# All weight blocks multiplied unsplit from a landing ring of eight, in a two-layer transformer kernel in 32-bit floats

## What is computed

```
x = layer_norm(ALPHA * x + s5_mixer(x), ...)              # state-space mixer with a scan over 256 steps
kv = shared_kv(x, ...)                                    # keys, values, two compressed branches
x = layer_norm(ALPHA * x + nsa_mixer(x, ..., kv), ...)    # 16 heads, 3 attention branches, gates
for l in range(2):
    h = rms_norm(x, g_mix)
    x = x + (retention_na_mixer(h) if l == 0 else diff_attention_mixer(h))
    x = x + cross_attention(rms_norm(x, g_x), memory)     # 4 heads, 256 memory rows
    gate, up = split(rms_norm(x, g_ffn) @ w_ffn_in)       # 2048 -> 2 x 5632
    x = x + (silu(gate) * up) @ w_ffn_out                 # 5632 -> 2048
```

## Time and profile before

| | |
|---|---|
| median of 3 runs | 3734.83 us (3734.79 to 3744.37) |
| the profiled execution's own time | 3741.45 us |
| its span, first to last instruction | 3739.7 us |
| TensorE busy (PE) | 3589.8 us, 96% |
| VectorE busy (DVE) | 2219.3 us, 59% |
| ScalarE busy (ACT) | 1654.8 us, 44% |
| mean granted TensorE clock | 0.983 of 2.4 GHz |
| read from memory | 607.85 MB, 163 GB/s over the span |

### The profile page before, as it was taken

The page is one execution under the profiler, slowest core; times in us unless marked ns, Lnnn a source line. Parts: engine busy times, 40 slices in busy tenths (PEclk is TensorE's granted clock), DMA queues, the critical chain, the costliest instruction groups (busy, mean ns, idle before and its releaser), DMA issues.

```text
span 3739.7 us, 48011 instructions
## 1 busy us (share of the span) xinstructions
PE 3589.8 (96%) x20133; PEld 3082.5 (82%) x20133; DVE 2219.3 (59%) x2922; ACT 1654.8 (44%) x2278; POOL 233.1 (6%) x236
## 2 busy tenths in 40 slices
PE   7888999999999999899999999999989999999999
PEld 6767788988977887778888888888877788888887
DVE  5997644655656655566555555555555665455554
ACT  4344434655645433455434434444433544344343
POOL 3562000000010020000000000000000000000000
PEclk9999999999999999999999999999998999999999
DMA  7334566555555664456656666566423466666664
GB/s 209 100 101 160 145 185 172 143 150 144 141 186 158 180 162 140 138 154 173 188 188 188 188 189 186 185 177 179 135 90 123 146 182 180 195 188 183 194 187 146
DMA packets 859479, 613.12 MB, mean 164 GB/s; under 512 B 10402, under 2 KB 752401, under 8 KB 858240
## 3 DMA queue, kind: packets, MB, share of 16 engines
q1 hardware_dynamic: 857168, 602.24, 55.2%
q0 software_dynamic: 2096, 7.81, 0.8%
HBM read 607.85 MB, written 2.16 MB: 163 GB/s over the span
## 4 chain that ended last, share of the span: by engine, by line
PE 83%; DVE 9%; ACT 3%; POOL 2%; issue 1%; SPq 0%; DMA 0%; DVEq 0%; ACTq 0%
PE acc L994 27%; PE acc L983 26%; PE acc L996 14%; PE acc L1006 9%; DVE wL L2070 3%; PE psC L1190 2%; PE psA L1159 1%; ACT wH L1473 1%; PE psA L1135 1%; DVE arena L2512 1%; POOL arena L806 1%; PE psB L1173 0%; ACT arena L1450 0%; POOL mem_v L792 0%; PE psC L1145 0%
## 5 line engine op out<-in xcount | busy, mean ns | idle before, releaser
L2070 DVE TENSOR_TENSOR wL<-ring,wH 128x1024 fp32r<-128x1024 f32 x1128 | 1346.2, 1235 | 984.9 <-ACT wH L1473 983.5
L1473 ACT CAST wH<-ring 128x1024 fp32r<-128x1024 f32 x1128 | 1126.2, 1047 | 1114.1 <-PE acc L996 532.7
L994 PE MATMUL acc<-act,wH 128*128 128x512 f32 x4480 | 1598.3, 401 | 8.7 <-DVE wL L2070 7.0
L996 PE MATMUL acc<-act,wL 128*128 128x256 f32 x4480 | 1258.0, 281 | 0.0
L994 PEld LDWEIGHTS acc<-act,wH 128*128 128x128 f32 x4480 | 844.2, 188 | 222.2 <-DVE wL L2070 8.7
L996 PEld LDWEIGHTS acc<-act,wL 128*128 128x128 f32 x4480 | 848.4, 189 | 2.7 <-issue 1.9
L1006 PE MATMUL acc<-act,wH 128*128 128x256 f32 x2560 | 482.0, 290 | 15.5 <-DVE wL L2070 15.5
L1006 PEld LDWEIGHTS acc<-act,wH 128*128 128x128 f32 x2560 | 408.4, 195 | 20.4 <-DVE wL L2070 17.2
L983 PE MATMUL acc<-wH,act 128*128 128x512 f32 x1152 | 372.0, 400 | 8.8 <-DVE act L2062 7.7
L983 PE MATMUL acc<-wH,hidH 128*128 128x512 f32 x960 | 369.1, 394 | 10.5 <-DVE outL L2062 5.3
L1006 PE MATMUL acc<-act,wL 128*128 128x256 f32 x1280 | 366.2, 286 | 0.0
(11 more groups left out here) (348 smaller groups left out, 2743.2 us busy)
## 6 DMA issues: line engine op xcount, KB each, us to landing
ring<-in_w_ffn_in SPq DMA_DIRECT2D x176, 1024.0 KB, 5.8
ring<-in_w_ffn_out SPq DMA_DIRECT2D x88, 1024.0 KB, 5.2
ring<-in_b_w_in SPq DMA_DIRECT2D x64, 1024.0 KB, 6.3
ring<-in_w_in_ab SPq DMA_DIRECT2D x56, 1024.0 KB, 5.5
ring<-in_w_in_c SPq DMA_DIRECT2D x48, 1024.0 KB, 5.8
ring<-in_kv_w SPq DMA_DIRECT2D x24, 1024.0 KB, 5.7
ring<-in_a_w_in SPq DMA_DIRECT2D x16, 1024.0 KB, 7.5
ring<-in_w_xkv SPq DMA_DIRECT2D x16, 1024.0 KB, 5.3
```

The source lines that it names most:

```text
L994: pe.matmul(bank.rearrange("p (h t) -> p h t", h=2), high[:, t, :], act2[:, t, :, :], start=t == 0, stop=False)
L996: ins = pe.matmul(bank[:, T:2 * T], low[:, t, :], xH[:, t, :], start=False, stop=t == ph.kt - 1)
L1473: act.copy(wH[:, split_slot, cols], ring[:, slot, cols]).then_inc(h_made, 1)
L2070: dve.tensor_tensor(wL[:, split_slot, cols], ring[:, slot, cols], wH[:, split_slot, cols].bitcast(F32), ALU.subtract).then_inc(l_made, 1)
```

## The change

- The ring has eight slots; `wH`, `wL` and all split tiles go, and so do ACT's 1128 casts and DVE's 1128 subtractions of weights. The type fp32r is not used any more.
- SyncE's queue may overwrite a slot once TensorE has finished its last block (`blocks_done`), up to seven blocks ahead of it. The first seven fetches after the constants now stand ahead of the fetch of `mem_2`; before, three did.
- TensorE waits for the landing of the block itself and forms one 32-bit matmul for each product: 16 of 256 columns for a feat block, 8 of 512 for a tok block. In the joined style the first eight tiles are summed in the left half of the bank and the other eight in the right half, so that ACT's copy and DVE's addition stay.
- Activations are held once (`act_in`, `hid_in`, `hid_top`, `gelu_in`, `xo_in`, `gate_kept`): ACT's copy stays, DVE's low part goes. In the feed-forward part DVE multiplies straight into `hid_in`, and an empty instruction (printed as ISA) counts it; ACT's extra copy goes.
- `rest_of_norm` on DVE waits for two more counts, its own centring and the eight transposes of the layer norm.

```diff
-SLOTS = 4
-SPLIT_SLOTS = 2
+SLOTS = 8
...
-            def fetch(src, ph, slot, number, first):
-
-                if first >= SLOTS:
-                    sp.wait_ge(l_made, number * 2 - 2 * (SLOTS - 1))
-                if first - SLOTS in W1_BLOCKS:
-                    sp.wait_ge(blocks_done, first - SLOTS + 1)
+            def fetch(src, ph, n):
+
+                slot = n % SLOTS
+                if n >= SLOTS:
+                    sp.wait_ge(blocks_done, n - SLOTS + 1)
                 dst = ring[:, slot, :]
...
-            for n in range(1, SLOTS):
-                fetch(at.src(0, n // 2, n % 2), at.kt, n, n, n)
+            for n in range(1, 8):
...
             sp.dma_start(hs, a["mem_2"][0].rearrange("(m p) d -> p m d", p=P)).then_inc(mem_landed, 16)
-            for n in range(SLOTS, 2 * SLOTS):
-                fetch(at.src(1, (n - SLOTS) // 2, n % 2), at.kt, n % SLOTS, n, n)
...
-                xH, xL = inputs_at.get(id(ph), (actH, actL))
-                if b == 0 and ph.chunk0 + c >= 2:
+                x = inputs_at.get(id(ph), act_in)
+                if b == 0 and ph.pair_uses(i, c) > 0:
                     pe.wait_ge(drained[ph.pair(c)], ph.pair_uses(i, c))
                 pair = acc[:, 2 * ph.pair(c):2 * ph.pair(c) + 2, :]
-                pe.wait_ge(l_made, ph.blocks_before(i, c, b) * 2 + 2)
-                s = ph.block(c, b) % SPLIT_SLOTS
-                high, low = (w[:, s, :].rearrange("p (t n) -> p t n", t=ph.kt) for w in (wH, wL))
+                number = ph.blocks_before(i, c, b)
+                pe.wait_ge(landed[number % SLOTS], 16 * (number // SLOTS + 1))
+                w = ring[:, number % SLOTS, :].rearrange("p (t n) -> p t n", t=ph.kt)
+                opens = i == c == b == 0
...
-                            rows = slice(m * P, (m + 1) * P)
-                            for n, (x, w) in enumerate(((xH, high), (xH, low), (xL, high))):
-                                ins = pe.matmul(pair[:, m, :], x[:, k, rows], w[:, t, :],
-                                                start=k == 0 and n == 0, stop=k == last_k and n == 2)
+                            ins = pe.matmul(pair[:, m, :], x[:, k, m * P:(m + 1) * P], w[:, t, :],
+                                            start=k == 0, stop=k == last_k)
                     if tiles is not None and tiles[-1] != ph.kt - 1:
                         return
                 elif ph.joined:
-                    bank = pair[:, b, :]
+                    half = ph.kt // 2
                     for t in range(ph.kt):
                         if late is not None:
                             late(t)
-                        if turn_call is not None and i == 0 and c == 0 and b == 0:
-                            pe.wait_ge(turned_l, FT * turn_call + t + 1)
-                        pe.matmul(bank.rearrange("p (h t) -> p h t", h=2), high[:, t, :], act2[:, t, :, :],
-                                  start=t == 0, stop=False)
-                        ins = pe.matmul(bank[:, T:2 * T], low[:, t, :], xH[:, t, :], start=False,
-                                        stop=t == ph.kt - 1)
+                        if turn_call is not None and opens:
+                            pe.wait_ge(turned_kept, FT * turn_call + t + 1)
+                        ins = pe.matmul(pair[:, b, t // half * T:(t // half + 1) * T], w[:, t, :], x[:, t, :],
+                                        start=t % half == 0, stop=t % half == half - 1)
                 else:
-
                     for f in range(ph.cols // P):
-                        dst = pair[:, 0, (b + f) * T:(b + f + 1) * T]
                         for t in range(ph.kt):
-                            if turn_call is not None and i == 0 and c == 0 and b == 0:
-                                pe.wait_ge(turned_l, FT * turn_call + t + 1)
-                            for n, (x, w) in enumerate(((xH, high), (xL, high), (xH, low))):
-                                ins = pe.matmul(dst, w[:, t, f * P:(f + 1) * P], x[:, t, :],
-                                                start=t == 0 and n == 0,
-                                                stop=t == ph.kt - 1 and n == 2)
+                            if turn_call is not None and opens:
+                                pe.wait_ge(turned_kept, FT * turn_call + t + 1)
+                            ins = pe.matmul(pair[:, 0, (b + f) * T:(b + f + 1) * T], w[:, t, f * P:(f + 1) * P],
+                                            x[:, t, :], start=t == 0, stop=t == ph.kt - 1)
...
-            def split_weights(slot, split_slot, number, landings, first, halves=(0, 1)):
-
-                act.wait_ge(landed[slot], landings)
-                if first >= SPLIT_SLOTS:
-                    act.wait_ge(blocks_done, number - (SPLIT_SLOTS - 1))
-                for k in halves:
-                    cols = slice(k * HALF, (k + 1) * HALF)
-                    act.copy(wH[:, split_slot, cols], ring[:, slot, cols]).then_inc(h_made, 1)
-
...
-                        act.activation(actH[:, k, :], bank, ACT.Identity, scale=scale).then_inc(turned_h, 1)
+                        act.activation(act_in[:, k, :], bank, ACT.Identity, scale=scale).then_inc(turned_kept, 1)
...
+                dve.wait_ge(ln_centred, MT * (D // COLS) * (l + 1))
+                dve.wait_ge(turned, 8 * (TURN_LN[l] + 1))
...
-            def split_weights(slot, split_slot, number):
-
-                for k in range(2):
-                    cols = slice(k * HALF, (k + 1) * HALF)
-                    dve.wait_ge(h_made, number * 2 + (k + 1))
-                    dve.tensor_tensor(wL[:, split_slot, cols], ring[:, slot, cols],
-                                      wH[:, split_slot, cols].bitcast(F32), ALU.subtract).then_inc(l_made, 1)
-
...
-                        dve.tensor_tensor(hid_f, hid_f, silu_g, ALU.mult).then_inc(drained[ffn_in.pair(1)], 1)
-
-                    def hidden_low(i):
-
+                        dve.tensor_tensor(hid_in[:, 2 * i:2 * i + 2, :], hid_f, silu_g, ALU.mult)\
+                            .then_inc(drained[ffn_in.pair(1)], 1)
                         dve.wait_ge(drained[ffn_in.pair(1)], ffn_in.pair_uses(i, 1) + 1)
-                        dve.wait_ge(hid_h, i + (pairs_done + 1))
-                        dve.tensor_tensor(hidL[:, 2 * i:2 * i + 2, :], hid_f, hidH[:, 2 * i:2 * i + 2, :].bitcast(F32),
-                                          ALU.subtract).then_inc(hid_l, 1)
+                        dve.engine_nop().then_inc(hid_kept, 1)
 
                     for i in range(ffn_in.iters):
```

More of the change, by code:

```diff
@@ L117, in __init__ @@
         assert kt * cols == SLOT
-        assert iters == 1 or (self.body * blocks % SLOTS == 0 and self.body % 2 == 0)
+        assert iters == 1 or self.body % 2 == 0
     def pair(self, c):
@@ L584, in drain_chunk @@
             fn(i, c, src).then_inc(drained[ph.pair(c)], 1)
[L587 to L593, removed]
+        SPLITS = [(gT, 8, gelu_in), (glT, 8, act_in), (oT, NH, act_in), (rgT, H8, hid_in),
+                  (nqT, H8, hid_in[:, H8:2 * H8, :]), (dqT, NH, hid_top)]
         S_GELU, S_GLU, S_NSA, S_RET, S_NA, S_DIF = range(6)
         def split_steps(upto):
-            return sum(n // 4 for _, n, _, _ in SPLITS[:upto])
+            return sum(n // 4 for _, n, _ in SPLITS[:upto])
         rows = [
@@ L653, in stream @@
                         for b in range(ph.blocks):
-                            n = ph.block(c, b)
-                            fetch(ph.src(i, c, b), ph.kt, n % SLOTS, ph.blocks_before(i, c, b), n)
+                            fetch(ph.src(i, c, b), ph.kt, ph.blocks_before(i, c, b))
             def stream_w1(ph, w):
@@ L660, in stream_w1 @@
                     n = ph.block0 + b
[L661 removed]
+                    fetch(w.rearrange("(j p) n -> p j n", p=P)[:, b * 16:(b + 1) * 16, :], 16, n)
             at = s5_u
[L664 removed]
+            fetch(at.src(0, 0, 0), at.kt, 0)
             for k in range(2):
@@ L1554, in cross_high @@
                 act.wait_ge(o_ready, u["n"] + 1)
-                act.activation(xoH[:, u["q_head"], :], psC[:, 0:T], ACT.Identity).then_inc(cross_highs, 1)
+                act.activation(xo_in[:, u["q_head"], :], psC[:, 0:T], ACT.Identity).then_inc(o_used, 1)
             def cross_attention(l, steps):
@@ L1875, in tail_act @@
                     opens = part == 0
-                    def cast(i, k):
-                        n = ffn_in.block(0, k) + 4 * i
-                        split_weights(n % SLOTS, n % SPLIT_SLOTS, n, 16 * (n // SLOTS + 1), n)
-                    def hidden_high(i):
-                        act.wait_ge(drained[ffn_in.pair(1)], ffn_in.pair_uses(i, 1) + 1)
-                        act.activation(hidH[:, 2 * i:2 * i + 2, :], hid_f, ACT.Identity).then_inc(hid_h, 1)
                     for i in range(ffn_in.iters):
-                        cast(i, 1)
                         if opens and i == 0:
@@ L2110, in cross_attention @@
                 next(blocks)
-                next(steps)
```

(21 more changed lines are left out.)

205 lines of the change are left out of this document (51 added, 154 removed).

## The result

The changed kernel takes 4383.09 us, median of 4 runs (4380.61 to 4385.93), against 3736.26 for the kernel before in the same comparison: a ratio of 1.1726, with a 95% interval from 1.1706 to 1.1747. It is 17.3% slower. The forecast was 4386.

What follows compares the result with a forecast made beforehand. The prediction took TensorE to bound the kernel: 3741.45 + 716 (products) + 1 (gate) - 28 - 12 - 10 - 15 = 4393 us, or 4386 us against the median, 17% slower. The range was 4320 to 4470 us.

Steps and rivals of the forecast that it cites:

- What bounds the kernel: Whole kernel: TensorE sets the time, busy 3589.8 of 3739.7 us; memory is ahead of the engines.
- The products: TensorE's 564 blocks: 3880 us as plain 32-bit matmuls against 3164 us as three fp32r matmuls, 716 us more.
- What goes with the splitting: TensorE's waits and slower clock: four savings expected from dropping the splitting, -28, -12, -10 and -15 us.
- weight lows: TensorE's waits for DVE's low parts of weights, 27.8 us, go wholly: -28 us.
- activation lows: TensorE's waits for DVE's low parts of activations, 24.3 us: half goes, -12 us; bounds 0 and -24.
- scan, POOL, softmax: TensorE's waits for results of these chains, 30.9 us: a third goes, -10 us; bounds 0 and -31.
- clock: TensorE's granted clock, lower at 50-500 and 2750-2850 us, rises as it idles less: -15 us; bounds 0 and -49.
- (a): Whole kernel: idle time stays and only the products change, 4452 us, or 4468 with a late `mem_2`; chance 0.12.
- (b): TensorE's idle time: all four savings at their far ends, -132 us, giving 4320 us; chance 0.04.
- (c): TensorE's products: the count of passes decides, 4/3 of the old products, about 4725 us; chance 0.02.
- (d): TensorE's products: 256 columns take 0.215 us in all, memory binds, 2794 us, faster than before; chance 0.02.
- Edits costed at nothing: Copies, half-bank sums, DVE's empty instruction, `rest_of_norm`'s waits, later `mem_2` fetch: 0 us; bounds for `mem_2` 0 and +16.

Runs made afterwards that it cites:

- fourth corner: Changed kernel without splitting, each product again three fp32r matmuls, weights from one fixed tile, ring of four, `mem_2` fetched where it was: 3640.06 us, ratio 0.9738.
- third experiment: Changed kernel without splitting, one fp32r matmul for each product, weights from one fixed tile, ring of four: 2210.65 us, ratio 0.5917.

## Why the prediction was right

**What bounds the kernel**, and that memory does not: right. The fetch queue waits for 4035 us, and half the ring can go. The signs named beforehand are there as well: 220.8 and 109.5 us for the two stretches, DVE below 900 us, ACT below 600, and 89 us of idle time where about 100 was forecast.

**The products.** Forecast 3880 us for the new ones; by the paces above, 364 x 6.90 + 200 x 6.85 = 3882. A pass of 256 columns takes 0.2156 us in runs of a thousand, as in the four passes of the earlier trace rows. The old ones were put at 3164; with the fourth corner's paces for joined and tok blocks (5.65, and 87.1 / 16 = 5.44) and the 5.76 of the earlier trace rows it is 3156, since each of the two tok stretches of the earlier trace rows held a wait of 0.7 us for a weight low. So the term was 726 and not 716. The runs add what no trace could: 678 us beside the splitting, 743 without it. The term is right as work of TensorE, but the time it adds depends on how much of it falls into idle time. Cover explains why it can be less than 726, not why it is 743 in the second case. The gate's cheaper products in the fourth corner are about 4 us of that; the rest is of the size of the 20 us that no row names above, and stays open with them.

**What goes with the splitting.** Forecast -65 in four terms, measured about -81:

| term | forecast | found | from |
|---|---|---|---|
| weight lows | -28 | -28 | no such wait is left |
| activation lows | -12 | -12 | 24.3 to 12.7 us |
| scan, POOL, softmax | -10 | -16 | 30.9 to 14.5 us; -14 with L1204 |
| clock | -15 | -20 | 1.7% of 3740 to 1.0% of 4382 |

Other, shorter waits make up the rest of the idle time's fall of 61 us. The clock's far end had been put at 49 us from two stretches alone; over the whole span the lower clock cost up to 64. The sum is 726 + 1 - 61 - 20 = 646, against 642 between the two spans. So the 3 us between forecast and result are partly luck: the products were some 10 us short and the idle terms some 16 us, with opposite signs.

The step that the experiments correct is the heading under which these terms stood. The prediction had them go with the splitting, and named longer blocks only for the clock. TensorE's idle time in us, and its granted clock, in the four kernels:

| | split | not split |
|---|---|---|
| three fp32r matmuls a product | 149.9, 0.983 | 96.2, 0.989 |
| one 32-bit matmul a product | 116.5, 0.991 | 89.1, 0.990 |

Longer blocks alone, with every cast and subtraction still made, took 33 of the 61 us of idle time, two thirds of the weight-low waits among them, and all of the clock term. The end of the splitting alone took 54 of the 61 us and most of the clock term. The two overlap: each removes a wait that the other would have removed too, so their effects must not be added.

**The rivals.** (a), that idle time stays and gives 4452 to 4468, fell: even with all splitting kept the time is 4414. (b), all terms at their far ends, would have been 4320; the wait for x and the chains stayed. (c), passes alone, 4/3 of the old products or 4725, fell with the pace of 0.2156 us. By the rule of the Trainium skill (FP8 and Floating Point Precision, TensorE Precision Notes) true FP32 is four passes. That the reduced form takes one is a reading of that section, which gives no count for it; the trace has one record for each fp32r matmul. For the full form the trace shows two records of 0.2156 us for 256 columns, which agrees with four passes in time, while the three reduced passes cost 0.353 us and not 0.32. The pace that (c) named as its condition was off: 4/3 of 3164 us is 0.234 us a pass of 256 columns and not 0.25. The measured 0.2156 is below both. (d), one pass doing for two, fell by the same rows. Its price was too high as well. The third experiment needs 2211 us with all fetches, so memory would not have bound: the products' 1940 us and the 571 us of other time (3735 less 3164) make 2511, some 280 below its 2794. The memory rate had been read from a stretch that did not ask for more, and the other time had been added to memory's, though fetches run beside it.

**Edits costed at nothing.** The order of `mem_2` (4385.5 against 4383) costs nothing that shows. The joined sums' new halves were not tried apart, but their block, 6.90 us, is 32 of the 0.2156 us passes with nothing over. `rest_of_norm`'s waits were not tried apart.

## What to carry to other kernels

Price a change of number format by the distance between starts in a run of the same shape, not by the count of passes and not by the duration of a record: here 0.43 us against 0.353, where counting would have said four against three. Engines that are not on the path may lose two thirds of their work (here DVE and ACT) and give back little time: 31 us beside the new products, up to 96 beside the old. What they give back is mostly the waits they caused, and dearer work on the bound engine hides part of those by itself. So a saving on a side engine has no price of its own; it depends on what the bound engine does meanwhile. Where a queue waits for free slots during the whole span, look there before making the ring deeper: here eight slots did no more than four.

## What the runs showed of the hardware that had not been expected

**A fixed cost of each fp32r matmul.** The timeline of PE in the kernel before, three matmuls of 512 columns to a pattern:

```profile
1443.37 0.61 PE L983 MATMUL acc<-wH,act 128*128 128x512 f32 x2
1443.82 0.39 PE L983 MATMUL acc<-wL,act 128*128 128x512 f32 x1
1444.05 0.61 PE L983 MATMUL acc<-wH,act 128*128 128x512 f32 x2
```

The pattern comes back after 0.68 us, 0.227 us a matmul of 512 columns. In the plain feat block a matmul of 256 columns takes 0.36 / 3 = 0.120 us. So 256 more columns cost 0.107 us, and twice that, 0.213, leaves 13 to 14 ns of each matmul that do not depend on the columns. In the joined block a pair of 512 and 256 columns takes 0.353 us where three times 0.107 are 0.32: some 16 ns for each of the two. A plain 32-bit pass of 256 columns takes 0.2156 us, 2 ns over twice 0.107. So the reduced form pays more for each matmul than the full one; at 13 to 16 ns for each of 17792 matmuls this is, as an estimate, 230 to 280 us of the old kernel. What causes it was not tried: each of these matmuls also has a weight load of its own, of 188 to 195 ns by the page, and that may set their pace as well as the type.

**Copies and subtractions beside matmuls cost them nothing where it could be read**: 5.65 us a joined block with DVE and ACT splitting 1 MB for each, and 5.65 us without; 4294.0 and 4293.0 us of busy TensorE in the two kernels with 32-bit products. **Memory** moved up to 366 GB/s in a slice of 55 us to one core, where the long stretches of the kernels shown here otherwise asked for 150 to 190.
